# Two transformer blocks in one program: the ends of all four attention stages are rearranged

## The chip, the core and the metric

The kernel runs on one core of one Trainium2 chip. It is one straight program for five engines: TensorE (PE, matmuls; its weight loads are PEld), VectorE (DVE), ScalarE (ACT), GpSimd (POOL) and SyncE (SP, which issues the loads). The metric is device time in microseconds (us), the median of the runs; lower is better.

## The reference

256 tokens of width 1024, batch 1, float32 in and out, four layers in a row; every layer is x + mixer(norm(x)) and x + MLP(norm(x)):

```python
# layer "even": 8 heads of neighbourhood attention (64 wide, window and bias) and 8 heads
#   of latent attention (96 wide keys, 64 wide values); both concatenated, then @ ev_w_o
# layer "odd": dilated attention, 16 heads, 3 groups of keys each, merged in one softmax; @ od_w_o
# second block, layer 0: gated convolution (1024) and memory attention (4 heads of 128) over
#   256 memory tokens; concatenated (1536), @ a_w_out
# second block, layer 1: forgetting attention (8 causal heads of 128 with a bias) and memory
#   attention (4 heads); concatenated (1536), @ b_w_out
sc = einsum('bqhd,bkhd->bhqk', q, k) * scale     # each head
p = softmax(sc + bias)
o = einsum('bhqk,bkhd->bqhd', p, v)
x = x + concatenate(o over heads) @ w_o
x = x + square(relu(norm(x) @ w1)) @ w2          # first block
x = x + 0.5 * (silu(h @ w_gate) * (h @ w_up)) @ w_down   # second block, before and after each mixer
```

## The kernel before

**Weights.** All weights stream through the core once, in 299 chunks of 1 MB. A chunk is loaded into one of two slots of `W_raw`, and then split so that float32 products come out of faster matmuls: ACT rounds it to `W_hi` (`split_hi`, L1041), DVE subtracts to get `W_lo` (`split_lo`, L1308), each in two halves, and PE multiplies activations and weights as hi\*hi, hi\*lo, lo\*hi (`three`, L680 to L682). `ahead(g, slot)` splits chunk g+1 while chunk g is multiplied; `split_hi(g)` first waits until chunk g-2 has been multiplied (`chunk_done`). SP loads a chunk as soon as the raw slot has been split.

**Order.** A list of stages (`make_plan`) is walked by each engine's program in the same order; within a stage the order is the order of the code, and semaphores join the engines. Each engine executes its own queue strictly in order: a waiting instruction holds up all behind it.

**Down stages.** An output projection is a stage of kind "down": `ev_o` and `od_o` with 4 chunks, `a_out` and `b_out` with 6. Chunk j covers 256 of the rows of the weight. Its activations are staged in a slot of `SX` as hi (ACT, `stage_hi`, L1108) and lo (POOL, L1866). Its 24 matmuls accumulate in banks 4 to 7 of the accumulator memory PS: the first token half t = 0 in banks 4 and 5, the second half t = 1 in banks 6 and 7 (12 matmuls each, `down_chunk`).

**Attention stages.** There are four: "even" (16 heads in 8 pairs), "dilated" (16 heads in 8 pairs), "memory0" (4 heads), "fox" (12 heads, each a unit of its own). The steps of a unit, each named by its helper:

- `scores` (PE, L787 and L794): q times k into banks 4 to 7;
- `soft` (DVE, L1353, L1356 or L1371): row maxima, and the biased scores where there is a bias;
- `exps` (ACT, L1115): exponentials and their row sums;
- `normalise` (DVE, L1379 and L1382): reciprocals of the sums, and probabilities times them;
- `transposes` (PE, L811): probabilities through the identity matrix into the lower banks;
- `keep_pt` (ACT, L1125): the transposed probabilities copied out of PS;
- `values` (PE, L828 and L837): v times probabilities;
- `output` (DVE, L1394): the result copied to where the projection reads it.

The first units' scores and `soft` (`open_attention`) are issued inside the last chunk of the projection stage ahead, between its matmuls. The results of that last chunk are taken out of PS by DVE ("last eviction": L1593 in even, four L1639 in dilated, L1324 and L1333 in memory0 and fox). PE starts the attention stage proper with `pe.wait_ge(acc_read, u0)`, a wait for that eviction. In memory0 DVE's `open_attention` first waits for POOL's last gated product of the convolution (`conv_cu_done`), since a buffer is shared. The down stage starts after the last `values`; its second chunk is split then.

## Time and profile before

| | |
|---|---|
| median of 3 runs | 1855.12 us (1854.73 to 1856.68) |
| the profiled execution's own time | 1857.85 us |
| its span, first to last instruction | 1856.0 us |
| PE busy | 1811.1 us, 98% of the span |
| DVE busy | 1209.7 us, 65% |
| ACT busy | 929.9 us, 50% |
| POOL busy | 285.9 us, 15% |
| share of PE in the chain that ended last | 92% |
| mean granted clock of TensorE | 0.991 |

All durations of rows come from the profiled execution. A matmul's duration holds a pipelined tail, so the pace is read from the starts of rows, not from their durations. The granted clock is a share of 2.4 GHz; 0.50 is the lower level, 1.2 GHz.

### The profile page before, as it was taken

The page shows a single profiled execution, that of the slowest core. Times are in us where ns is not written, and L with a number is a line of the kernel's source. Part 1 is how long each engine was busy: PE and PEld are TensorE (multiplying, and loading weights), DVE is VectorE, ACT ScalarE, POOL GpSimd, SP SyncE. Part 2 cuts the span into 40 slices and gives each one's busy share as a digit, 9 for nine tenths or more (in the row PEclk, how much of TensorE's full clock was granted, in tenths as well). Part 3 has the DMA queues.
Part 4 walks back from the last instruction along what each step waited for, and adds up shares of the span by engine and source line. Part 5 has one row for each costly group of instructions (what it writes and reads, how often), then busy time and mean ns, then how long its engine had stood idle before and what let it go on. Part 6 is the DMA issues. An engine that isn't in the chain of part 4 may idle for free.

```text
span 1856.0 us, 27676 instructions
## 1 busy us (share of the span) xinstructions
PE 1811.1 (98%) x9835; PEld 1529.4 (82%) x9835; DVE 1209.7 (65%) x1536; ACT 929.9 (50%) x1396; POOL 285.9 (15%) x249
## 2 busy tenths in 40 slices
PE   9899999999989999999999989999999999899998
PEld 7678888888867888888888878888888888788886
DVE  6867745867876665566647756665667656656664
ACT  5465445434356444555545445454564445555543
POOL 1010021211201002110023920002000311020012
PEclk9899999999999999999999999999999999999999
DMA  6335555555523555555555535555556555245553
GB/s 222 109 131 182 182 198 171 174 181 183 180 92 103 182 182 202 189 174 189 194 187 178 189 129 181 181 189 196 182 174 209 184 186 187 81 148 184 193 188 136
DMA packets 215146, 320.19 MB, mean 173 GB/s; under 512 B 6040, under 2 KB 167072, under 8 KB 214944
## 3 DMA queue, kind: packets, MB, share of 16 engines
q1 hardware_dynamic: 214048, 315.80, 51.1%
q0 software_dynamic: 736, 3.15, 0.4%
q8 instruction: 48, 0.79, 0.2%
q10 hardware_dynamic: 288, 0.23, 0.0%
q14 instruction: 26, 0.21, 0.0%
HBM read 318.11 MB, written 1.06 MB: 172 GB/s over the span
## 4 chain that ended last, share of the span: by engine, by line
PE 92%; DVE 3%; ACT 2%; issue 1%; DMA 1%; POOL 0%; DVEq 0%; SPq 0%; POOLq 0%; ACTq 0%
PE PS L675 26%; PE PS L680 14%; PE PS L681 14%; PE PS L682 14%; PE PS L673 13%; PE PS L669 4%; PE PS L670 2%; PE PS L828 1%; PE PS L787 1%; DVE W_lo L1308 1%; PE PS L749 1%; PE PS L811 1%; DMA W_raw<-in_ev_w_in 1%; ACT U L1115 1%; ACT U L1125 1%
## 5 line engine op out<-in xcount | busy, mean ns | idle before, releaser
L1308 DVE TENSOR_TENSOR W_lo<-W_raw,W_hi 128x1024 fp32r<-128x1024 f32 x598 | 771.7, 1330 | 279.8 <-ACT W_hi L1041 258.1
L675 PE MATMUL PS<-XN,W_hi 128*128 128x512 f32 x2072 | 738.5, 396 | 0.0
L1041 ACT ACTIVATE W_hi<-W_raw 128x1024 fp32r<-128x1024 f32 x598 | 598.5, 1050 | 173.8 <-PE PS L682 116.8
L673 PE MATMUL PS<-XN,W_lo 128*128 128x256 f32 x2072 | 578.3, 279 | 0.0
L675 PEld LDWEIGHTS PS<-XN,W_hi 128*128 128x128 f32 x2072 | 388.8, 188 | 79.9
L673 PEld LDWEIGHTS PS<-XN,W_lo 128*128 128x128 f32 x2072 | 390.6, 189 | 13.5
L680 PE MATMUL PS<-W_hi,SX 128*128 128x512 f32 x780 | 305.1, 391 | 1.7 <-DVE W_lo L1308 1.7
L682 PE MATMUL PS<-W_hi,SX 128*128 128x512 f32 x780 | 303.8, 389 | 0.0
L681 PE MATMUL PS<-W_lo,SX 128*128 128x512 f32 x780 | 303.7, 389 | 0.0
L1866 POOL TENSOR_TENSOR SX<-U,SX 128x512 fp32r<-128x512 f32 (+1 forms) x98 | 128.6, 1316 | 1094.3 <-ACT SX L1108 1094.3
L1054 ACT ACTIVATE T<-PS 128x512 f32<-128x512 f32 x152 | 91.0, 599 | 405.2 <-PE PS L675 405.1
L1324 DVE TENSOR_TENSOR T<-PS,T 128x512 f32<-128x512 f32 x128 | 88.5, 691 | 213.6 <-ACT T L1054 213.6
L1108 ACT ACTIVATE SX<-U 128x512 fp32r (+2 forms) x98 | 60.5, 629 | 235.8 <-PE PS L682 232.3
L680 PEld LDWEIGHTS PS<-W_hi,SX 128*128 128x128 f32 x780 | 147.1, 189 | 32.7 <-issue 2.4
L681 PEld LDWEIGHTS PS<-W_lo,SX 128*128 128x128 f32 x780 | 147.1, 189 | 30.5
L682 PEld LDWEIGHTS PS<-W_hi,SX 128*128 128x128 f32 x780 | 146.8, 188 | 30.4
L680 PE MATMUL PS<-W_hi,XN 128*128 128x512 f32 (+1 forms) x352 | 138.5, 393 | 1.9 <-DVE W_lo L1308 1.2
L682 PE MATMUL PS<-W_hi,XN 128*128 128x512 f32 (+1 forms) x352 | 136.6, 388 | 0.0
L681 PE MATMUL PS<-W_lo,XN 128*128 128x512 f32 (+1 forms) x352 | 136.6, 388 | 0.0
L669 PE MATMUL PS<-XN,W_hi 128*128 128x512 f32 x296 | 118.6, 401 | 1.2 <-DVE XN L1338 1.2
L670 PE MATMUL PS<-XN,W_lo 128*128 128x256 f32 x296 | 82.2, 278 | 0.0
L680 PEld LDWEIGHTS PS<-W_hi,XN 128*128 128x128 f32 x352 | 66.1, 188 | 17.3 <-DVE W_lo L1308 3.3
(169 smaller groups left out, 1499.7 us busy)
## 6 DMA issues: line engine op xcount, KB each, us to landing
W_raw<-in_ffn_w_gate_up SPq DMA_DIRECT2D x88, 1024.0 KB, 5.1
W_raw<-in_mlp_w SPq DMA_DIRECT2D x64, 1024.0 KB, 5.2
W_raw<-in_ffn_w_down SPq DMA_DIRECT2D x44, 1024.0 KB, 4.9
W_raw<-in_od_w_in SPq DMA_DIRECT2D x36, 1024.0 KB, 5.1
W_raw<-in_a_w_in SPq DMA_DIRECT2D x14, 1024.0 KB, 5.0
W_raw<-in_mem_w_kv SPq DMA_DIRECT2D x8, 1024.0 KB, 5.1
W_raw<-in_w_kvf SPq DMA_DIRECT2D x8, 1024.0 KB, 5.4
W_raw<-in_ev_w_in SPq DMA_DIRECT2D x6, 1024.0 KB, 5.3
```

What stands on the lines that cost most here:

```text
L669: mm(bank, wT(W_hi, slot, k, fb), both, start=True, stop=False)
L670: mm(bank[:, S:], wT(W_lo, slot, k, fb), xn[:, k, 0, :], start=False, stop=False)
L673: mm(bank[:, S:], wT(W_lo, slot, k, fb), xn[:, k, 0, :], start=False, stop=False)
L675: last = mm(bank, wT(W_hi, slot, k, fb), both, start=False, stop=k == KD - 1)
L680: mm(bank, xh, wh, start=start, stop=False)
L681: mm(bank, xh, wl, start=False, stop=False)
L682: return mm(bank, xl, wh, start=False, stop=stop)
L1041: A(W_hi[:, slot, halves(h)], W_raw[:, slot, halves(h)], ACT.Copy).then_inc(w_hi, 1)
L1054: A(T0[:, pair, :].rearrange("p (f t) -> p f t", f=2), PS[:, 2 * pair:2 * pair + 2, S:2 * S], ACT.Copy, scale=times).then_inc(cross_out, 1)
L1308: V.tensor_tensor(W_lo[:, slot, halves(h)], W_raw[:, slot, halves(h)], W_hi[:, slot, halves(h)], ALU.subtract).then_inc(w_lo, 1)
L1324: return V.tensor_tensor(dst.rearrange("p (f t) -> p f t", f=2), PS[:, 2 * pair:2 * pair + 2, 0:S], T0[:, pair, :].rearrange("p (f t) -> p ...
L1866: nc.gpsimd.tensor_tensor(SX[:, slot, 1, 0:st["ks"] * S], down_src(st, j), SX[:, slot, 0, 0:st["ks"] * S], ALU.subtract).then_inc(st_lo, 1)
```

## The change

1. **Opening.** DVE normalises the first two heads before it does the last eviction. ACT computes their exponentials before its own part: in even and dilated ACT now evicts the second half of the last result (`v_kept`), DVE the first. PE's wait for the eviction moves from the front of the stage to just ahead of the first `values`; to allow it, transposes use the banks that the last projection does not occupy (`free`), `values` the others (`taken`).
2. **Interleaving.** The first chunk of the output projection is multiplied inside the attention stage, in two halves of 12 matmuls (`down_half`): in even and dilated both halves between the last units' steps, in memory0 and fox three halves (chunk 0 twice, chunk 1 once; the fourth follows the stage). So `stage_early` stands further ahead on ACT, and chunk 1 is split within the stage.
3. **Around it.** In memory0 the first two chunks of `a_out` are staged in the stage ahead (ACT), and POOL makes their lo part before the last quarter of the convolution. `soft` of heads 2 and 3 waits for the convolution's product there, no longer heads 0 and 1. The order of ACT and DVE within even changes: ACT does the exponentials of units 1 and 2 after unit 0 is kept and before unit 1 is kept. The loops of the four down stages are written out.

```diff
+                late = (st["u"] - 1) % 2
+                st["free"], st["taken"] = 2 - 2 * late, 2 * late
...
-            def down_chunk(st, g, staged, slot, first, final):
+            def down_chunk(st, g, staged, slot, first, final, tiles=range(TT), last_half=True):
...
+            def down_half(st, j, t, last_half):
+                down_chunk(st, st["g"] + j, st["staged0"] + j + 1, (st["g"] + j) % 2, j == 0,
+                           j == st["n"] - 1, (t,), last_half)
...
                 elif kind == "attend":
-                    pe.wait_ge(acc_read, u0)
...
+                    def accumulators_read():
+                        pe.wait_ge(acc_read, u0)
+                        if st["paired"]:
+                            pe.wait_ge(v_kept, st["v_kept"])
+                    if st["name"] == "even":
+                        for u in us:
+                            for n_ in units[u]:
+                                transposes(n_)
+                            if u + 2 in us:
+                                scores(u + 2)
+                            if u == us[0]:
+                                accumulators_read()
+                            if u >= us[-2]:
+                                down_half(then, 0, u % 2, u == us[-1])
+                            values(u)
+                    elif st["name"] == "dilated":
+                        for u in us:
+                            if u + 1 in us:
+                                scores(u + 1)
+                            else:
+                                pe.wait_ge(s_soft, a0 + m)
+                                down_half(then, 0, 0, False)
+                            transposes(units[u][0])
+                            if u == us[0]:
+                                accumulators_read()
+                            transposes(units[u][1])
+                            if u == us[-1]:
+                                down_half(then, 0, 1, True)
+                            values(u)
...
@@ ACT, even
+                        exps_unit(us[0])
+                        act.wait_ge(chunk_done, g0)
+                        A(region(R["na_v"] + 512, 512), PS[:, st["taken"] + 1, :], ACT.Copy,
+                          scale=rstd_of(1)).then_inc(v_kept, 1)
+                        keep_unit(us[0])
+                        exps_unit(us[1])
+                        exps_unit(us[2])
+                        for u in us[1:]:
+                            keep_unit(u)
+                            exps_unit(u + 2)
+                            if u == us[-4]:
+                                stage_early(then)
+                            if u == us[-2]:
+                                ahead(then["g"], then["g"] % 2)
...
@@ DVE, open_attention
-                if st["name"] == "memory0":
-                    dve.wait_ge(conv_cu_done, 4)
                 soft(st["a0"])
                 soft(st["a0"] + 1)
+                normalise(st["a0"])
+                normalise(st["a0"] + 1)
...
@@ DVE, memory0
+                        second_chunk()
+                        dve.wait_ge(conv_cu_done, 4)
+                        soft_unit(us[2])
+                        soft_unit(us[3])
+                        output(us[0])
+                        output(us[1])
+                        normalise_unit(us[2])
+                        normalise_unit(us[3])
...
@@ POOL, convolution
+                        if c == 3:
+                            for j in range(2):
+                                slot = (then["g"] + j) % 2
+                                pool.wait_ge(st_hi, then["staged0"] + j + 1)
+                                Pg.tensor_tensor(SX[:, slot, 1, :], down_src(then, j), SX[:, slot, 0, :],
+                                                 ALU.subtract).then_inc(st_lo, 1)
```

What this makes of the queues is shown at three places. First DVE at the start of the even stage, before (ISA rows are `soft`, L1593 is the last eviction, L1379 and L1382 are `normalise`):

```order
L1371 ISA U,ST<-PS,U 128x256
L1371 ISA ST 128x1
L1593 TENSOR_SCALAR U<-PS,ST 128x512 x2
L1371 ISA U,ST<-PS,U 128x256
L1371 ISA ST 128x1
...
L1379 RECIPROCAL ST<-ST 128x2
L1382 TENSOR_SCALAR U<-U,ST 128x256 x2
```

and after (L1490 is `soft`, L1498 and L1501 `normalise`, L1712 the eviction):

```order
L1490 ISA U,ST<-PS,U 128x256
L1490 ISA ST 128x1
L1498 RECIPROCAL ST<-ST 128x2
L1501 TENSOR_SCALAR U<-U,ST 128x256 x2
L1498 RECIPROCAL ST<-ST 128x2
L1501 TENSOR_SCALAR U<-U,ST 128x256 x2
L1712 TENSOR_SCALAR U<-PS,ST 128x512
L1490 ISA U,ST<-PS,U 128x256
```

The two normalisations moved ahead of the eviction and of the second unit's `soft`, and the eviction is one instruction, not two.

Second, PE in memory0 from the end of the last projection to the first matmul of `a_out`, before (L787 scores, L811 transposes, L828 values):

```order
L787 MATMUL PS<-U 128x256 x2
L811 MATMUL PS<-K,T 128x128 x4
L787 MATMUL PS<-U 128x256 x2
L828 MATMUL PS<-U 128x256 x2
L811 MATMUL PS<-K,U 128x128 x4
L828 MATMUL PS<-U 128x256 x2
L811 MATMUL PS<-K,U 128x128 x4
L828 MATMUL PS<-U 128x256 x2
L811 MATMUL PS<-K,T 128x128 x4
L828 MATMUL PS<-U 128x256 x2
L680 MATMUL PS<-W_hi,SX 128x512
```

and after (L824 transposes, L800 scores, L841 values, L691 to L693 the halves of chunks 0 and 1, 12 matmuls each):

```order
L824 MATMUL PS<-K,U 128x128 x8
L691 MATMUL PS<-W_hi,SX 128x512
...
L800 MATMUL PS<-U 128x256 x4
L841 MATMUL PS<-U 128x256 x4
L691 MATMUL PS<-W_hi,SX 128x512
...
L824 MATMUL PS<-K,T 128x128 x4
L824 MATMUL PS<-K,U 128x128 x4
L691 MATMUL PS<-W_hi,SX 128x512
...
L841 MATMUL PS<-U 128x256 x4
```

Between any two groups of attention work that depend on each other through ACT or DVE there now stand 12 matmuls of the projection.

Third, POOL at the last quarter of the convolution, before (L1907 the gated product, L1914 and L1918 the taps, L1919 the result):

```order
L1919 TENSOR_TENSOR U<-U 128x512
L1907 TENSOR_TENSOR U<-T 128x2x256
L1914 TENSOR_SCALAR U<-U,G 128x256 x4
L1918 TENSOR_TENSOR U<-U 128x512
L1914 TENSOR_SCALAR U<-U,G 128x256 x2
```

and after (L2061 the lo parts of the first two chunks of `a_out`):

```order
L2076 TENSOR_TENSOR U<-U 128x512
L2061 TENSOR_TENSOR SX<-U,SX 128x512 x2
L2064 TENSOR_TENSOR U<-T 128x2x256
L2071 TENSOR_SCALAR U<-U,G 128x256 x4
L2075 TENSOR_TENSOR U<-U 128x512
```

The two subtractions, and with them a wait for ACT's staging, stand ahead of the last product and all of its taps.

## Rows read from the trace of the kernel before

**Rows 1.** Timeline, even, PE: start, duration, engine, line, operation, count, idle before

```profile
73.64 0.39 PE L682 MATMUL PS<-W_hi,XN 128*128 128x512 f32 x1
77.80 1.94 PE L811 MATMUL PS<-K,U 128*128 128x128 f32 x8 [3.76 <-DVE U L1382]
...
83.53 1.09 PE L811 MATMUL PS<-K,U 128*128 128x128 f32 x8
...
85.70 1.08 PE L828 MATMUL PS<-U 128*64 128x256 f32 x8
...
105.58 1.08 PE L828 MATMUL PS<-U 128*64 128x256 f32 x8 [1.84 <-ACT U L1125]
...
108.52 1.08 PE L828 MATMUL PS<-U 128*64 128x256 f32 x8 [0.83 <-ACT U L1125]
109.54 0.50 PE L680 MATMUL PS<-W_hi,SX 128*128 128x512 f32 x1
```

**Rows 2.** Windows: length, busy of PE, PEld, DVE, ACT, POOL, clock, DMA

```profile
74.03:109.54 35.51, 28.49 (x178) 19.76 (x177) 26.34 (x97) 24.66 (x78) 2.50 (x2) 0.90 0.06 25
528.11:576.14 48.03, 40.28 (x569) 31.08 (x568) 34.34 (x115) 32.13 (x92) 2.63 (x2) 0.93 0.02 8
1068.15:1081.23 13.08, 7.93 (x41) 5.99 (x41) 7.83 (x21) 7.55 (x21) 5.68 (x5) 1.00 0.06 23
1596.10:1629.71 33.61, 27.32 (x128) 21.63 (x129) 21.44 (x79) 20.31 (x61) 2.49 (x2) 0.85 0.00 1
...
1599.00:1602.36 3.36, 3.35 (x12) 2.95 (x13) 2.25 (x11) 1.51 (x5) 0.00 (x0) 0.50 0.00 0
1622.84:1629.30 6.46, 5.58 (x15) 4.44 (x16) 1.45 (x3) 2.49 (x3) 1.64 (x2) 0.50 0.01 3
```

**Rows 3.** Timeline, even, ACT: exponentials and copies of transposed probabilities

```profile
74.23 0.18 ACT L1115 ACTIVATION_READ_ACCUMULATOR U<-U,ST 128x1 f32 x1
...
82.60 0.51 ACT L1115 ACTIVATE U<-U,ST 128x256 f32<-128x256 f32 x1 [2.23 <-DVE ST L1371]
...
84.59 1.06 ACT L1125 ACTIVATE U<-PS 128x512 f32<-128x512 f32 x2
```

**Rows 4.** Timeline, even, DVE: the first head's normalisation

```profile
77.04 0.61 DVE L1382 TENSOR_SCALAR U<-U,ST 128x256 f32<-128x256 f32 x2
```

**Rows 5.** Timeline, dilated, PE

```profile
527.72 0.39 PE L682 MATMUL PS<-W_hi,XN 128*128 128x512 f32 x1
...
537.49 1.08 PE L828 MATMUL PS<-U 128*64 128x256 f32 x8 [0.35 <-ACT U L1125]
...
538.97 1.13 PE L787 MATMUL PS<-U 64*128 64x256 f32 x8
...
542.86 1.08 PE L828 MATMUL PS<-U 128*64 128x256 f32 x8 [0.41 <-ACT U L1125]
...
572.04 0.87 PE L811 MATMUL PS<-K,T 128*128 128x128 f32 x6 [0.81 <-DVE T L1382]
...
574.67 1.08 PE L828 MATMUL PS<-U 128*64 128x256 f32 x8 [0.46 <-ACT U L1125]
...
576.14 0.50 PE L680 MATMUL PS<-W_hi,SX 128*128 128x512 f32 x1
```

**Rows 6.** Timeline, a_out, ACT: staging released by the ends of two chunks

```profile
1087.26 0.63 ACT L1108 ACTIVATE SX<-U 128x512 fp32r x1 [5.03 <-PE PS L682]
...
1092.70 0.63 ACT L1108 ACTIVATE SX<-U 128x512 fp32r x1 [2.91 <-PE PS L682]
```

**Rows 7.** Timeline, memory0, DVE normalising a head

```profile
1070.49 1.43 DVE L1382 TENSOR_SCALAR T<-T,ST 128x256 f32<-128x256 f32 x2
```

**Rows 8.** Timeline, memory0, POOL's last step of the convolution

```profile
1069.91 1.59 POOL L1919 TENSOR_TENSOR U<-U 128x512 f32<-128x512 f32 x1
```

**Rows 9.** Waits of PE, fox: total us, times, longest

```profile
PE PS L811 <- DVE U L1333: 2.9, 1, 2.9
PE PS L828 <- ACT U L1125: 2.8, 3, 1.2
```

More of the change, by code:

```diff
@@ L348, in build_program @@
         bias_ready = sem("bias_ready")
+        v_kept = sem("v_kept")
         dve_chain, pool_chain = sem("dve_chain"), sem("pool_chain")
@@ L723, in down_chunk @@
                 chunk_ready(g, 0 if by_half else 1)
-                for t in range(TT):
-                    if first and t == 1 and st["src"] == "h" and not st["each"]:
-                        pe.wait_ge(h_done, st["h0"])
+                for t in tiles:
                     steps = [(ks, b) for ks in range(ks_n) for b in range(2)]
@@ L730, in down_chunk @@
                     for at, (ks, b) in enumerate(order):
-                        if by_half and t == 0 and ks and not any(k for k, _ in order[:at]):
+                        if by_half and t == tiles[0] and ks and not any(k for k, _ in order[:at]):
                             chunk_ready(g, 1)
@@ L1012, in _ @@
                     a0, m = st["a0"], len(st["what"])
[L1014 to L1029 removed]
+                    us, then = st["units"], st["next_down"]
@@ L1275, in _ @@
                     a0, m = st["a0"], len(st["what"])
-                    if stages[stages.index(st) - 1]["kind"] != "up":
-                        exps(a0)
-                    exps(a0 + 1)
-                    if st["name"] == "even":
-                        exps(a0 + 2)
-                        exps(a0 + 3)
-                    lead = 2 if st["name"] in ("memory0", "fox", "even") else 1
-                    for u in st["units"]:
+                    us, then = st["units"], st["next_down"]
```

218 lines of the change are left out of this document (157 added, 61 removed).

## The prediction

> **What bounds the kernel now.** I read the shares of busy time first: PE is busy for 98% of the span and makes up 92% of the chain that ended last. So only PE's own idle time, and time in which its clock is low, can be won. Next came the granted clock by stretches, then PE's waits and its timeline in the four attention stages. These stages take 35.5, 48.0, 13.1 and 33.6 us with PE busy for 28.5, 40.3, 7.9 and 27.3 us [rows 2]: 26.2 us idle in 130. Their mean clock is 0.90, 0.93, 1.00 and 0.85. Even, dilated and fox each open with a long wait, followed by work at 0.50: even waits 3.76 us for the first normalisation, which stands behind the eviction on DVE [rows 1]; fox waits 2.9 us and then works at 0.50 for 3.4 us [rows 2, 9]. The ends look alike: the last units have no further scores to cover ACT's copy, so PE waits 1.84 and 0.83 us in even [rows 1], 0.81 and 0.46 us in dilated [rows 5], and in fox the clock falls again for 6.5 us, into the first down chunk [rows 2].
>
> The work of PE is the same after the change: the half chunks only stand elsewhere. The sum is therefore what goes of waits and low clock, less new waits. A chunk takes 5.44 us (the ends of two chunks, 1087.26 and 1092.70 [rows 6]), a half 2.7 us.
>
> **Even.** The last projection matmul ends at 74.03 (73.64 and its 0.39 [rows 1]). ACT's exponentials of the first two heads end at 74.4 already [rows 3]. Normalising a head is a reciprocal and two multiplies, 0.8 us by my estimate with the 0.61 of the two multiplies in it [rows 4]; the second head is ready at 75.2 and, with the 0.15 us from there to PE (77.04 plus 0.61 to 77.80 [rows 1, 4]), its transposes go at 75.4. Transposes and scores take 2.17 us in all (83.53 to 85.70 [rows 1]), of which about 0.5 are the second head's transposes; so the first values start near 76.9. The eviction, one half on each engine, is over by then.
>
> Then the order on ACT costs something. ACT keeps unit 0 until 76.9 (1.06 [rows 3]), computes unit 1 until 78.9 (four exponentials are 1.99, 82.60 to 84.59 [rows 3]), DVE normalises until 79.7 and only then does unit 2's `soft`, whose first head is ready some 0.7 us later; ACT computes unit 2 from 80.4 to 82.4, and only then keeps unit 1, until 83.5. PE, queued behind, waits at the transposes (about 1.4 us) and at the values of unit 1 (2.3 us), which start at 83.5 instead of 85.70 [rows 1]. So of 3.76 us of wait and the low clock 2.2 us are left as gain. At the end 1.84 and 0.83 go, covered by a half chunk each, and moving the staging ahead of a keep that PE is waiting for costs its 1.06 us (two copies at 0.53; the 0.63 of rows 6 has a tail). Sum: 2.2 + 2.67 - 1.06 = **3.8 us**. Bounds: 2.1 if the low clock returns in these waits (below), 8.9 if none of the new waits came.
>
> **Dilated.** The last matmul ends at 528.11 and the first values start at 537.49 [rows 5]. Afterwards scores, transposes and values follow at once, with both heads normalised and the eviction shared between DVE and ACT (about 1.5 us each, four half-height instructions divided by two). In the next unit the way from scores to values is 3.89 us (538.97 to 542.86, its wait of 0.41 included [rows 5]), so the values start near 532.1: 5.4 us won. The repeated part stays as it is. At the end 0.81 and 0.46 go behind two half chunks: 1.3 us. Sum **6.7 us**; bounds 5.5 (one more 1.2 us wait for the second head) and 7.5.
>
> **Memory0.** 13.08 us with 7.93 busy [rows 2]: 5.15 us of waits, and a half chunk now stands between every pair of steps that wait for each other. The wait for chunk 1's split is covered: ACT starts it near 70, DVE ends near 73.5, PE comes to it near 76. What may stay is the DVE's pace. POOL's last product and taps now start after staging and two subtractions, some 9 us later, and run beside DVE's normalisations. The row that shows such a meeting: two multiplies take 1.43 us beside POOL's 1.59 us instruction [rows 7, 8], where they take 0.61 alone [rows 4]. For the two heads that PE waits for at the front that is up to 1.6 us, of which I take 0.35, since the product is nearly over. Sum **4.8 us**; bounds 1.9 (each of the four normalisations slowed by 0.8) and 5.2.
>
> The Trainium skill ("SBUF — State Buffer", section "Who interferes with whom") says that VectorE in its two-port modes and GpSimd take one pair of ports as a lock, and that the one that comes second is blocked until the first ends. The trace agrees for the one meeting above: the multiplies end 0.4 us after POOL's instruction. By the rule every normalisation in memory0 could be held by one instruction of POOL, which would take the sum to the lower bound just named; by the row alone it stays near 4.8.
>
> **Fox.** Waits of 2.9 and 2.8 us [rows 9]; at 0.50 the work in the two low stretches, 3.35 and 5.58 us busy [rows 2], takes twice as long, so half of 8.93, 4.5 us, is lost there. Together 10.2 us. New: unit 2 has neither its maxima nor its probabilities ahead, since they stand behind the eviction, `soft` of units 2 and 3 and one set of exponentials on ACT: about 1.2 us of wait, and 0.3 us at the first head. At the end three half chunks, 8.2 us, cover the copies and the split of chunk 1. Sum **8.7 us**; bounds 5.9 (the second fall of the clock stays) and 9.9.
>
> **Edits at nothing.** The written-out loops add no work. POOL's later convolution ends near 82; its result is wanted by the staging of chunk 3, near 87. Chunk 2 of each projection is split when chunk 0 is done, up to one half chunk and one values step before PE needs it; in memory0 its first half is ready about 1 us early. If that cover were gone it would cost 1 us a stage. Chunk 3 is loaded earlier than before, into a DMA queue that is idle in these stages (0.00 to 0.06 busy [rows 2]).
>
> **Sum.** 3.8 + 6.7 + 4.8 + 8.7 = 24.0 us. Against the profiled execution: span 1856.0 to 1832.0, and with the 1.85 us around it (1857.85 less 1856.0) 1833.85. That execution was 2.73 us above the median; from the median 1855.12 the same gain gives **1831.1 us**.
>
> **The rivals.**
> - *The clock falls in even all the same.* For it: in fox it fell at 1622.84 after waits of no more than 1.2 us each [rows 2, 9], and even now has waits of 0.9, 0.5 and 2.3 us close together. Against: memory0, idle for 5.15 of 13.08 us, stayed at 1.00 [rows 2]. Price: 3.4 us at 0.50 lose 1.7, 6.5 us lose 2.8 (half the busy time of the two stretches [rows 2]). Time 1832.8 to 1833.9. The Trainium skill ("TensorE: Matmul & The Clock Gate", section "A second HAM failure mode: psum-queue depth-cycling") tells of a kernel whose frequent short idles between groups of matmuls made the clock go down and up; the row of fox agrees, that of memory0 does not.
> - *POOL slows memory0* to its lower bound: 2.9 us less, 1834.0. With the one above 1836 to 1837.
> - *Only the ends are won.* Were the first values no earlier in any stage (another wait, the eviction say, in place of the normalisation), what remains is 2.7 - 1.1 in even, 1.3 in dilated, half of the 5.15 in memory0, and 2.8 of waits plus 2.8 of clock in fox: 11 us, 1844. Against it: the eviction ends ahead of the first values in each walk above.
> - *Slower: the half chunks run at the low clock.* If the changed rhythm keeps the clock at 0.50 where they stand, each of the ten halves costs 2.7 us more, 27 us, against 24 won: 1858. It decides from the point at which nine of ten halves are hit. Against it: a half chunk is solid work, and the clock came back to 1.00 after 3.4 and 6.5 us each time [rows 2].
>
> **Chances.** Forecast 0.57; clock in even 0.17; POOL 0.12, either alone or with the clock; only the ends 0.06; slower 0.02; the rest, 0.06, for more won than worked out (fewer new waits in even and fox, up to 4 us). About 0.2% (3.7 us) is what a measurement of this kernel can tell from no change. Faster by more 0.95, within 0.03, slower 0.02. The range takes in both clock and POOL at its upper end, 1837.5, and the rest at its lower end, 1827.0.
>
> **What the profile after would show.** Right: the four stages, from the last projection matmul to the first matmul of the remaining down stage, less the half chunks, at about 31.7, 41.3, 8.3 and 24.9 us (rows 2 less the sums); no wait above 0.6 us before the first values; a granted clock of 1.00 in dilated and fox; in even two waits near 80 and 82, of some 1.4 and 2.3 us, the second for ACT's copy. Wrong: a wait of PE for POOL's or ACT's staging ahead of a half chunk; chunk 2 late behind DVE's last output; a clock of 0.50 beside half chunks; first values where they were.

## The result, and the profile after

The changed kernel takes **1833.3 us** (median of 4 runs, 1832.19 to 1833.82), the kernel before on the same chip 1855.9 us (4 runs, 1854.73 to 1859.20). The ratio is 0.9875, 95% interval 0.986 to 0.989: 1.25% faster, inside the range given, 2.2 us above the forecast of 1831.1.

The profiled execution took 1833.31 us, with a span of 1831.5 us: 24.5 less than before. PE is busy for 1800.1 us of it, where it was busy for 1811.1. The matmuls are the same 9835, so most of these 11.0 us are matmuls that no longer run at half clock; the other 13.5 are idle time of PE. Of the 11.0, 1.4 lie between 50 and 60 us, where even starts no earlier for it (73.91 against 74.03). In the four attention stages the gain is 9.9 us of half clock and 14.4 of idle time.

The four attention stages as in [rows 2], from the end of the last projection matmul to the first matmul of the down stage that is left (columns as there):

```profile
73.91:112.24 38.33, 33.26 (x200) 23.67 (x200) 28.03 (x96) 26.86 (x81) 2.52 (x3) 0.96 0.07 25
525.32:571.59 46.27, 43.08 (x592) 33.25 (x592) 34.07 (x112) 35.46 (x96) 3.11 (x3) 1.00 0.08 26
1058.15:1075.52 17.37, 15.67 (x77) 12.81 (x77) 11.74 (x22) 8.59 (x21) 11.73 (x10) 1.00 0.26 99
1582.24:1612.34 30.10, 28.21 (x161) 24.37 (x159) 21.11 (x73) 20.30 (x59) 2.83 (x3) 1.00 0.10 36
```

The stages are longer by the half chunks that now stand in them (2.72 us each: two in even and dilated, three in memory0 and fox). PE's idle time in them is 5.07, 3.19, 1.70 and 1.89 us; it was 7.02, 7.75, 5.15 and 6.29. The clock of the first is 0.96, of the others 1.00. Less the half chunks:

| stage | before | forecast | after | won, forecast | won, measured |
|---|---|---|---|---|---|
| even | 35.51 | 31.7 | 32.89 | 3.8 | 2.6 |
| dilated | 48.03 | 41.3 | 40.83 | 6.7 | 7.2 |
| memory0 | 13.08 | 8.3 | 9.21 | 4.8 | 3.9 |
| fox | 33.61 | 24.9 | 23.05 | 8.7 | 10.6 |

In fox [rows 2] reach four matmuls into the first down chunk, some of them at half clock; the table goes to the same matmul after, at 1613.45. The stages sum to 24.3 of the 24.5 us: nothing of weight happened outside them.

Even after, PE; the rows answer to [rows 1]:

```profile
73.52 0.39 PE L693 MATMUL PS<-W_hi,XN 128*128 128x512 f32 x1
74.20 0.66 PE L824 MATMUL PS<-K,U 128*128 128x128 f32 x4 [0.29 <-DVE U L1501]
...
76.83 1.08 PE L841 MATMUL PS<-U 128*64 128x256 f32 x8
78.51 0.66 PE L824 MATMUL PS<-K,U 128*128 128x128 f32 x4 [0.59 <-DVE U L1501]
...
83.24 1.11 PE L841 MATMUL PS<-U 128*64 128x256 f32 x8 [2.03 <-ACT U L1198]
...
112.24 0.51 PE L691 MATMUL PS<-W_hi,SX 128*128 128x512 f32 x1
```

The first values of the kernel before, to compare with the row at 76.83:

```profile
81.67 1.93 PE L828 MATMUL PS<-U 128*64 128x256 f32 x8
```

The wait of 3.76 us is gone; the first values start 2.92 us after the projection's end (7.64 before). But those of unit 1 wait 2.03 us for ACT's copy, L1198. And fox, where [rows 9] had 2.9 us in front and 2.8 at the end:

```profile
1584.44 0.92 PE L841 MATMUL PS<-U 128*128 128x256 f32 x4 [0.24 <-DVE U L1452]
1586.95 0.66 PE L824 MATMUL PS<-K,T 128*128 128x128 f32 x4 [1.59 <-DVE T L1501]
```

These two are all the waits of the stage that are long enough to be listed; the end has none. In dilated the first values start 3.85 us after the projection's end at 525.32:

```profile
529.17 1.08 PE L841 MATMUL PS<-U 128*64 128x256 f32 x8 [0.45 <-ACT U L1198]
```

Memory0 keeps three waits, all for DVE's normalisation (L1501):

```profile
1058.89 0.66 PE L824 MATMUL PS<-K,U 128*128 128x128 f32 x4 [0.74 <-DVE U L1501]
1059.82 0.66 PE L824 MATMUL PS<-K,U 128*128 128x128 f32 x4 [0.27 <-DVE U L1501]
...
1070.01 0.66 PE L824 MATMUL PS<-K,T 128*128 128x128 f32 x4 [0.61 <-DVE T L1501]
```

### The profile page after: what moved, and what is told of

The parts are those of the page before. It is cut to its first block, busy times and chain, and to the rows that moved or that the text cites. A ratio compares the mean times of both kernels' runs of the same rounds, so it can differ in the third digit from the quotient of the medians.

```text
span 1831.5 us, 27590 instructions
## 1 busy us (share of the span) xinstructions
PE 1800.1 (98%) x9835; PEld 1523.3 (83%) x9835; DVE 1209.1 (66%) x1533; ACT 932.5 (51%) x1399; POOL 285.5 (16%) x249
## 3 DMA queue, kind: packets, MB, share of 16 engines
HBM read 318.11 MB, written 1.06 MB: 174 GB/s over the span
## 4 chain that ended last, share of the span: by engine, by line
PE 92%; DVE 4%; ACT 2%; issue 1%; DMA 1%; POOL 0%; DVEq 0%; ACTq 0%; POOLq 0%
PE PS L686 26%; PE PS L691 14%; PE PS L693 14%; PE PS L692 14%; PE PS L684 13%; PE PS L680 4%; PE PS L681 2%; DVE W_lo L1427 2%; PE PS L841 1%; PE PS L800 1%; PE PS L762 1%; PE PS L824 1%; ACT U L1188 1%; PE PS L961 1%; ACT U L1198 0%
## 5 line engine op out<-in xcount | busy, mean ns | idle before, releaser
L1427 DVE TENSOR_TENSOR W_lo<-W_raw,W_hi 128x1024 fp32r<-128x1024 f32 x598 | 771.3, 1329 | 264.6 <-ACT W_hi L1111 242.5
L684 PEld LDWEIGHTS PS<-XN,W_lo 128*128 128x128 f32 x2072 | 391.0, 189 | 13.5
L691 PE MATMUL PS<-W_hi,SX 128*128 128x512 f32 x780 | 305.1, 391 | 1.8 <-DVE W_lo L1427 1.7
L693 PE MATMUL PS<-W_hi,SX 128*128 128x512 f32 x780 | 303.3, 389 | 0.0
L691 PEld LDWEIGHTS PS<-W_hi,SX 128*128 128x128 f32 x780 | 146.5, 188 | 32.5 <-issue 2.4
L693 PEld LDWEIGHTS PS<-W_hi,SX 128*128 128x128 f32 x780 | 146.5, 188 | 30.3
L691 PE MATMUL PS<-W_hi,XN 128*128 128x512 f32 (+1 forms) x352 | 138.6, 394 | 3.4 <-issue 1.5
L693 PE MATMUL PS<-W_hi,XN 128*128 128x512 f32 (+1 forms) x352 | 136.7, 388 | 0.0
L691 PEld LDWEIGHTS PS<-W_hi,XN 128*128 128x128 f32 x352 | 66.1, 188 | 18.7 <-DVE W_lo L1427 3.3
```

The lines of the kernel that those rows point to most:

```text
L684: mm(bank[:, S:], wT(W_lo, slot, k, fb), xn[:, k, 0, :], start=False, stop=False)
L691: mm(bank, xh, wh, start=start, stop=False)
L693: return mm(bank, xl, wh, start=False, stop=stop)
L1427: V.tensor_tensor(W_lo[:, slot, halves(h)], W_raw[:, slot, halves(h)], W_hi[:, slot, halves(h)], ALU.subtract).then_inc(w_lo, 1)
```

## The experiments

All are edits of the changed kernel; u is a unit, us the units of a stage. Since one edit moves the time by less than the runs scatter, I read each first from the length of its stages. Stage lengths less the half chunks in them, to the first matmul of the down stage in fox too (31.57 before):

| kernel | even | dilated | memory0 | fox | median us |
|---|---|---|---|---|---|
| changed | 32.89 | 40.83 | 9.21 | 21.94 | 1833.3 |
| changed, again | 31.45 | 40.87 | 9.22 | 21.92 | 1833.51 |
| opening only | 36.18 | 42.51 | 14.51 | 22.73 | 1842.35 |
| ends only | 33.84 | 45.23 | 13.92 | 24.46 | 1845.73 |
| even, both edits | 29.31 | 40.86 | 9.19 | 23.59 | 1831.38 |
| fox without lead | 31.48 | 40.83 | 9.23 | 24.99 | 1835.7 |
| without taps | 31.47 | 40.86 | 8.47 | 21.94 | 1831.43 |
| fox, three heads | 31.48 | 40.86 | 9.23 | 20.12 | 1831.1 |
| memory0 staged earlier | 32.89 | 40.85 | 7.93 | 21.93 | 1832.86 |
| filler matmuls | 31.47 | 40.85 | 9.22 | 23.64 | 1832.91 |
| even and fox | 29.27 | 40.87 | 9.23 | 20.11 | 1828.40 |
| all three edits | 29.29 | 40.85 | 7.93 | 20.16 | 1827.49 |

Where an edit does not touch a stage, the length repeats to 0.05 us, except for two jumps: even 31.5 or 32.9, and fox 21.9 or 23.6. Both are the clock: it is 0.96 in the even of 32.9 us and 1.00 in that of 31.5, 0.95 in the fox of 23.6 us and 1.00 in that of 21.9.

### The changed kernel again

No edit.

> The changed kernel itself once more. What is open is whether the half clock of 3.4 us in even (1.7 us lost, from 84.2 us on) belongs to the kernel or to the single execution: the same instructions of that stage in the run without the lead in fox showed the same waits and full clock. If it belongs to the waits (2.03 us at 83), it falls again at the same place; if it is of the execution, it may fall there or not, with even at 31.5 or 32.9 us, and the time stays within 1832 to 1834.5.

The times were 1832.23 to 1833.92. The window 80 to 90 us, first in the trace of the changed kernel, then in this one (columns as above):

```profile
80.00:90.00 10.00, 7.97 (x45) 5.69 (x44) 7.20 (x31) 6.40 (x21) 0.00 (x0) 0.83 0.00 0
```

```profile
80.00:90.00 10.00, 7.74 (x55) 5.54 (x54) 8.20 (x36) 7.56 (x27) 0.00 (x0) 1.00 0.00 0
```

With the same instructions and the same wait (2.04 us at 83) the clock was 0.83 once and 1.00 once: so the fall belongs to the execution and not to the kernel alone. 0.83 over ten microseconds are 3.4 us at half speed, and the stage pays 1.44 us for them. Of the seven traces that left this place unedited, it fell there in three (changed, opening only, memory0 staged earlier).

### Opening only

```diff
-                            if u >= us[-2]:
-                                down_half(then, 0, u % 2, u == us[-1])
...
-                            if u == us[-4]:
-                                stage_early(then)
                             if u == us[-2]:
-                                ahead(then["g"], then["g"] % 2)
+                                stage_early(then)
+                        ahead(then["g"], then["g"] % 2)
```

and so in all four stages.

> The changed kernel with the half chunks undone: the first down chunk or chunks of each following stage, ACT's split and staging and DVE's second chunk go back behind the last heads; the heads normalised ahead of the last eviction, ACT's eviction of the second half and the transposes of fox one unit ahead stay. Theory (the two parts save apart, at the two ends of each stage, and add): the end waits of before come back, about 2.5 us in even, 1.5 in dilated, 2.5 in memory0 and 3.5 in fox, 10 in all, so about 1843 us, with the first values of every stage where the changed kernel has them (3.3 us after the stage's start in even, 3.9 in dilated). Rival (the half chunks are worth nothing of their own, the opening does it all): stages within 0.5 us of the changed kernel's, about 1834. Second rival (the parts need each other, since a gap at either end drops the clock): over 14 us slower, about 1848.

1842.35 us (1840.13 to 1844.21; ratio to before 0.9909, 0.9891 to 0.9928), 9 us above the changed kernel, near the 10 of the first theory. The parts are distributed otherwise. Memory0, first wait and last values:

```profile
1072.84 0.66 PE L824 MATMUL PS<-K,T 128*128 128x128 f32 x4 [3.18 <-DVE T L1478]
...
1074.27 3.57 PE L841 MATMUL PS<-U 128*128 128x256 f32 x8
```

DVE's normalisation of head 2 is waited for with 3.18 us (0.61 with a half chunk in front of it), and the eight values behind it take 3.57 where they take 1.89 at full clock: 5.3 us in that stage, twice what I expected. In even the wait of 1.84 us at the end is back, and behind it another 3.4 us at half clock. Fox loses only 0.8, against 3.5 expected. Its end has one wait, though no half chunk covers it now:

```profile
1612.91 0.66 PE L824 MATMUL PS<-K,T 128*128 128x128 f32 x4 [0.40 <-DVE T L1478]
```

So something other than the half chunks removes most of the 2.8 us of end waits of fox.

### Ends only

```diff
-                normalise(st["a0"])
-                normalise(st["a0"] + 1)
...
-                        for t in range(1 if st.get("next_attend") else TT):
+                        for t in range(TT):
...
-                        act.wait_ge(chunk_done, g0)
-                        A(region(R["na_v"] + 512, 512), PS[:, st["taken"] + 1, :], ACT.Copy,
-                          scale=rstd_of(1)).then_inc(v_kept, 1)
```

> The changed kernel with the opening undone: the first heads are normalised behind the last eviction, DVE evicts both halves, PE waits for both before its first attention work; the half chunks between the last heads' steps and the transposes of fox one unit ahead stay. Theory: the start waits of before come back, in dilated the 5.4 us that its stage saved at the front, in even 1 to 3.5 (the front wait comes back, but the clock that fell there in the changed kernel may stay up), in memory0 about 2.3, in fox 2.9 and up to 1.7 of half clock behind it: 12 to 14 us, so 1845 to 1847 us. Rival (the end waits carry the gain): under 5 us slower, 1838. In fox the steady period of three units stays 5.44 us, since the transposes one unit ahead are still there; if it goes back to 6.31, what shortened it was the opening.

1845.73 us (1845.36 to 1847.15; ratio 0.9933, 0.9915 to 0.9951), 12.4 above the changed kernel. The front waits are back, in memory0 with 3.65 us:

```profile
1067.15 1.09 PE L824 MATMUL PS<-K,U 128*128 128x128 f32 x4 [3.65 <-issue]
1068.73 1.11 PE L824 MATMUL PS<-K,U 128*128 128x128 f32 x4 [0.49 <-DVE U L1491]
```

The groups of four transposes take 1.1 us instead of 0.66: half clock behind the wait. Nine of the twelve matmuls of the half chunk behind them are slow too (0.43 us from start to start instead of 0.23): a half chunk does not bring the clock back at once. The total is as expected, but memory0 loses 4.7 us, twice the 2.3 expected, and dilated 4.4 for 5.4. Three units of fox take 5.44 us here too, so the opening is not what shortened them.

The two parts alone win 13.6 and 10.2 us from the 1855.9 of the first comparison, 23.8 together, where the whole wins 22.6. Against the kernel before as it ran beside them (1858.1) they win 15.7 and 12.3, 28.0 together. The transposes of fox one unit ahead are in both and count twice (2 to 3 us, next experiment), which leaves 21 to 26. So each part wins by itself, but whether they add up exactly these times do not decide, and no run separates the pieces of the opening (normalising first, the shared eviction, the later wait of PE).

### Fox without the lead

In the changed kernel PE issues the transposes of unit u + 1 and the scores of unit u + 4 ahead of the values of unit u. The loop of before did not:

```diff
-                        transposes(a0)
-                        scores(us[3])
...
-                            if u + 1 in us:
-                                transposes(units[u + 1][0])
-                            if u + 4 in us:
-                                scores(u + 4)
+                            transposes(units[u][0])
+                            if u + 3 in us:
+                                scores(u + 3)
```

> The changed kernel with the transposes of fox in their own unit again (one wait for the exps is added ahead of one half chunk), everything else kept. Theory (in the kernel before each unit of fox waited some 0.29 us for ACT's keep inside the step from transposes to values, too short for the list of waits, and the transposes one unit ahead hide it): the steady period of three units goes from 5.44 back to about 6.3 us, +2.6 us over nine units, about 1836. Rival (the period was shortened by the clock or by waits at the front that the opening took away): the period stays at 5.44 and the time within 0.5 us of 1833.

1835.7 us (1834.57 to 1836.52), 2.2 to 2.4 above; fox is 3.05 us longer. Two values steps in a row in the steady part, PE; first the changed kernel, then this one:

```profile
1591.14 0.82 PE L800 MATMUL PS<-U 128*128 128x128 f32 x4
1591.79 0.82 PE L841 MATMUL PS<-U 128*128 128x256 f32 x4
1592.45 0.60 PE L824 MATMUL PS<-K,T 128*128 128x128 f32 x4
1592.88 1.03 PE L800 MATMUL PS<-U 128*128 128x256 f32 x4
1593.75 0.82 PE L841 MATMUL PS<-U 128*128 128x256 f32 x4
```

```profile
1590.27 0.82 PE L800 MATMUL PS<-U 128*128 128x128 f32 x4
1591.21 0.89 PE L841 MATMUL PS<-U 128*128 128x256 f32 x4
1591.94 0.60 PE L824 MATMUL PS<-K,T 128*128 128x128 f32 x4
1592.38 1.03 PE L800 MATMUL PS<-U 128*128 128x256 f32 x4
1593.32 1.10 PE L841 MATMUL PS<-U 128*128 128x256 f32 x4
```

From scores to values 0.94 us pass without the lead, 0.65 with it, and no row shows an idle time (between the end of the scores and the values 0.12 us are left). ACT's row in that step, from the same trace:

```profile
1590.47 0.60 ACT L1196 ACTIVATE U<-PS 128x512 f32<-128x512 f32 x1 [0.49 <-PE PS L824]
```

ACT's copy ends at 1591.07 and the values that read it start at 1591.21, while the scores before them are over. With the lead the copy has been made a unit earlier. The period of three units is 6.31 us (1587.01 to 1593.32), against 5.44 in the changed kernel, and as in the kernel before (1605.67 to 1611.98):

```profile
1605.67 1.10 PE L828 MATMUL PS<-U 128*128 128x256 f32 x4
...
1611.98 1.10 PE L828 MATMUL PS<-U 128*128 128x256 f32 x4
```

The theory stands. Of the 3.05 us, 1.12 are listed waits (1.22, 0.33, 0.62 and 0.78 here against 0.24 and 1.59); the other 1.9 are 0.29 us a unit over some seven units. At the end of the stage two of the waits come back, 0.62 us ahead of a half chunk and this one:

```profile
1612.87 1.10 PE L841 MATMUL PS<-U 128*128 128x256 f32 x4 [0.78 <-ACT U L1196]
```

So of the 2.8 us at the end of fox the half chunks without the lead leave 1.40, and the lead without the half chunks left 0.40.

### Even, both edits

```diff
+                        exps_unit(us[1])
                         act.wait_ge(chunk_done, g0)
...
-                        exps_unit(us[1])
...
-                            exps_unit(u + 2)
-                            if u == us[-4]:
+                            if u == us[-3]:
                                 stage_early(then)
+                            exps_unit(u + 2)
...
+                if st["name"] == "even":
+                    soft(st["a0"] + 2)
+                    soft(st["a0"] + 3)
```

> The changed kernel with two edits in the stage even alone: the softmax and the exps of unit 1 are done ahead of the last eviction, and ACT's early staging stands one exps earlier, between keep(5) and exps(7). Theory: the second values waited 2.03 us for ACT's keep of unit 1 behind exps of unit 1, and 1.3 of it go; the wait of 1.15 at the early staging goes to 0 to 0.2; and if the clock does not fall at 84 us, 1.7 more: even shorter by 2.3 to 4.0 us (from 32.9 less its half chunks), 1829.5 to 1831. Rival (ACT's chain in front is only moved ahead of the eviction, which then comes later): the first values come 0.7 later and the sum is -1.0. Second rival for the clock: the gap of 2 us is not what lowers it, and the half clock shows in even also where the wait is gone.

Even is 29.31 us, 3.6 shorter than in the first trace and 2.15 shorter than at full clock. PE:

```profile
75.04 1.38 PE L824 MATMUL PS<-K,U 128*128 128x128 f32 x8 [1.11 <-DVE U L1501]
...
77.96 1.08 PE L841 MATMUL PS<-U 128*64 128x256 f32 x8 [0.47 <-ACT U L1198]
...
81.63 1.08 PE L841 MATMUL PS<-U 128*64 128x256 f32 x8 [0.50 <-ACT U L1198]
...
102.86 1.08 PE L841 MATMUL PS<-U 128*64 128x256 f32 x8 [0.39 <-ACT U L1198]
```

The 2.03 us became 0.50, at the price of first values 1.1 us later (4.02 us after the start; the rival's part, with 0.7 expected), and the 1.15 us at the early staging became 0.39. But the time fell only to 1831.38 (1829.50 to 1831.60), and the trace shows why: in this execution the clock was low in fox, which took 23.59 instead of 21.94 (without the three half chunks that stand in the length below):

```profile
1578.67:1610.42 31.75, 29.86 (x160) 25.65 (x159) 21.15 (x73) 20.32 (x59) 2.83 (x3) 0.95 0.11 34
```

### Fox with three heads ahead

```diff
+                                if st["next_attend"]["name"] == "fox":
+                                    exps(st["next_attend"]["a0"] + 2)
...
+                if st["name"] == "fox":
+                    soft(st["a0"] + 2)
...
+                if st["name"] == "fox":
+                    normalise(st["a0"] + 2)
```

> The changed kernel with one edit in fox alone: head 2 as well gets its softmax, exps and normalisation ahead of the last eviction (three heads instead of two). Theory (the 1.59 us in front of the transposes of head 2 wait for DVE's normalisation, which stands behind the eviction and its split only by its place in the queue): the wait goes, or 0.3 of it is left, fox less its half chunks goes from 21.9 to 20.4 us, about 1831.8. Rival (DVE is late in front anyway, so head 2's work delays the eviction and head 0): the same 1.5 us show up as a wait in front of the first values and fox stays at 21.9.

1831.1 us (1830.22 to 1831.76). The window of fox, to be read against the fourth row above:

```profile
1581.21:1609.49 28.28, 27.97 (x160) 24.32 (x159) 19.79 (x69) 19.40 (x55) 2.83 (x3) 1.00 0.11 38
```

0.31 us idle of 28.28: the wait of 1.59 is gone and nothing took its place. The theory stands to 0.3 us (20.12 for 20.4).

### Memory0 without the last taps, and with earlier staging

```diff
-                        for tap in (2, 1, 0):
+                        for tap in (2, 1, 0) if c < 3 else ():
```

> The changed kernel without the taps of POOL's convolution in its last quarter (six multiply-adds of the last quarter are left out, so its sum is not formed); everything else kept. Theory (POOL's multiply-adds slow DVE's rows beside them): DVE's split L1427 at 1062 takes 2.35 instead of 3.38 us, the normalisation that PE waits for last comes earlier and the wait of 0.61 goes: memory0 0.6 shorter, about 1832.7; the waits of 0.74 and 0.27 in front stay, since the subtractions of L2061 run there. Rival (DVE is slowed by PE's and ACT's accesses, or by its own operands' layout): the row stays at 3.4 us and memory0 at 9.2. Second rival (a POOL row of one kind slows DVE and of the other not): the rows beside L2061 stay slow and those beside L2071 are as slow as alone already.

DVE's second split in memory0 (L1427) and the normalisation that PE waits for last, with POOL's taps beside the split; the changed kernel:

```profile
1063.35 3.73 POOL L2071 TENSOR_SCALAR U<-U,G 128x256 f32<-128x256 f32 x2
...
1062.09 3.38 DVE L1427 TENSOR_TENSOR W_lo<-W_raw,W_hi 128x1024 fp32r<-128x1024 f32 x2 [1.01 <-ACT W_hi L1111]
...
1067.84 2.12 DVE L1501 TENSOR_SCALAR T<-T,ST 128x256 f32<-128x256 f32 x2
```

and without the taps:

```profile
1060.99 2.36 DVE L1427 TENSOR_TENSOR W_lo<-W_raw,W_hi 128x1024 fp32r<-128x1024 f32 x2 [1.00 <-ACT W_hi L1111]
...
1066.16 0.62 DVE L1501 TENSOR_SCALAR T<-T,ST 128x256 f32<-128x256 f32 x2
```

The split loses 1.02 us and the normalisation 1.50 to POOL. The last wait of PE goes, memory0 is 0.74 shorter (0.6 expected), and the front waits 1.30 where it waited 0.74 and 0.27: POOL's subtractions and product are still there. The theory stands. The second experiment moves them:

```diff
+                            if kind == "up" and s == 0 and st.get("next_attend", {}).get("name") == "memory0":
+                                stage_early(st["next_attend"]["next_down"])
...
-                                if st["next_attend"]["name"] == "memory0":
-                                    stage_early(st["next_attend"]["next_down"])
```

> The changed kernel with one edit ahead of memory0: ACT's early staging (the subtraction operands that POOL waits for) stands one chunk of the up projection earlier. Theory (what slows DVE in memory0, 3.4 us for a row that takes 2.35 alone, and the waits of 0.74, 0.27 and 0.61 of PE, are POOL's rows beside it, and POOL began when ACT's staging came, its wait of 6.85 us): POOL is done some 5 us earlier, the last wait of 0.61 goes and the front loses half: memory0 less its half chunks from 9.2 to 8.2 us or a bit over, about 1832.3. Rival (POOL's rows only move and meet other DVE rows of the up projection, whose splits feed PE): memory0 shortens, but the same time is lost ahead of it, and the total does not move. Second rival (ACT's staging delays ACT's own work there): a wait of PE of up to 2.7 us appears ahead of memory0, 1835.

```profile
1053.09 1.99 PE L800 MATMUL PS<-U 128*128 128x256 f32 x8 [1.69 <-DVE U L1452]
...
1060.06 0.66 PE L824 MATMUL PS<-K,U 128*128 128x128 f32 x4 [0.35 <-DVE U L1501]
...
1069.85 0.66 PE L824 MATMUL PS<-K,T 128*128 128x128 f32 x4 [0.20 <-DVE T L1501]
```

Memory0's waits fall from 1.62 to 0.55 us and the stage by 1.28, but the wait for the first scores, ahead of it, grows from 0.89 to 1.69. The distance from the end of dilated to the start of memory0 is 487.35 us here and 486.55 in the repetition. Net 0.5: the theory holds for the stage, the first rival for the account. The median moved by 0.4 to 0.7, which these runs alone would not show. POOL's two last taps L2071 take 2.46 us here, beside two short rows of DVE (0.69 us each), and 3.73 beside the split: both engines are slowed where they meet, not the later one alone. The split itself is not faster here but slower, beside POOL's last two rows of 1.29 and 2.13 us:

```profile
1062.33 4.48 DVE L1427 TENSOR_TENSOR W_lo<-W_raw,W_hi 128x1024 fp32r<-128x1024 f32 x2 [0.90 <-ACT W_hi L1111]
```

What shortens the last wait to 0.20 us is the normalisation behind it, which is back at 0.62 us.

The Trainium skill ("SBUF — State Buffer", section "Who interferes with whom") says that a VectorE instruction with two operands in SBUF, such as this split, contends with a GpSimd instruction that reads SBUF. The runs agree: 3.38 us with the taps, 2.36 without.

### Filler matmuls in the gap

```diff
+                        def filler(n):
+                            for _ in range(n):
+                                mm(PS[:, st["taken"] + 1, :], XN[:, 0, 0, 0:P], both_halves(XN, 0),
+                                   start=True, stop=True)
...
+                            if u == us[1]:
+                                filler(7)
```

> The changed kernel with seven extra matmuls whose result is not used, on PE, in the wait of 2.03 us ahead of the values of unit 1 in even; seven of these take 1.6 us at 0.23 us each. In the traces of that stage so far, with the same wait of 2.03 to 2.04 us, the clock fell behind it in three of seven and stayed at full in four. Theory (the idle gap is what lets the clock fall): with the gap filled it does not fall in even, the values start where they did, 9.3 us after the stage's start, and even is 36.9 us long; the times are 1832.2 to 1832.6 more often than 1833.3 to 1833.9. Rival (the gap has nothing to do with it): the half clock shows at 84 us in this trace too, or the times keep their mean of 1833.2. Second rival (the extra matmuls cost by themselves, since they end after the keep is ready): the values start up to 0.4 later.

```profile
81.27 1.91 PE L1045 MATMUL PS<-XN 128*128 128x512 f32 x7
83.38 1.08 PE L841 MATMUL PS<-U 128*64 128x256 f32 x8 [0.20 <-ACT U L1204]
```

The gap is filled and the values are not late. The clock stayed at 1.00 in even, as the theory wants, but so it did in four of seven traces with the gap. The times (1831.96, 1832.07, 1833.75, 1833.96) fall in the same two groups as without filler, since the clock fell in fox instead in the profiled execution. By itself it did not settle the cause. In even the clock was low behind the gap of 2.0 us in 3 of 7 traces, and in none of the 4 without that gap (both edits, even and fox, all three, filler); in fox it was low in 2 of 7 with the wait of 1.59 us, and in none of 3 without it. Such splits are weak: falls spread over the traces at random would give the first one time in five, the second one time in two.

The thirteen traces hold more, if every wait of PE above 1 us from 45 us on is set beside the clock. All low stretches, but for the one at the very end of the program, begin in such a wait or within 1.4 us behind it:

| wait of PE, us | waits | clock fell behind |
|---|---|---|
| 1.11 to 1.15 | 11 | 0 |
| 1.22 to 1.30 | 3 | 1 |
| 1.52 to 1.84 | 19 | 3 |
| 2.03 to 2.29 | 21 | 8 |
| 2.91 to 3.77 | 8 | 8 |

So the clock falls behind waits, the more often the longer they are, and behind each of the longest, which in the kernel before stood at the front of even, dilated and fox (3.76, 3.14 and 2.91 us). These are counts of thirteen executions and no rule.

### The edits together

> The same without the edit of memory0: even and fox alone. Theory: even 34.75, fox 28.3, memory0 as in the changed kernel at 17.4: 1829.4, 0.4 to 0.5 above the three together. Rival (the earlier staging of memory0 is worth its whole 1.3 us, and the 0.8 lost ahead of it in the single run was a half clock): 1830.3, 1.3 above. The clock: where the wait of 2.0 us at 83 us is gone, it does not fall in even in this trace either.

> The changed kernel with the three edits together: both softmaxes of units 0 and 1 and their exps ahead of the eviction in even and its staging one exps earlier, three heads ahead in fox, and the early staging of memory0 one chunk earlier. Theory (they act in different stages and add, at full clock): even 36.9 to 34.75, fox 30.1 to 28.3, memory0 17.4 to 16.1 less 0.8 lost ahead of it: 4.4 us below the 1833.4 of the changed kernel, 1829.0. Rival (the clock takes back part of it: each trace so far lost 0, 1.7 or 3.4 us in one or two stretches, and a stage saved may start one elsewhere): 1830.5 to 1831.5.

Even and fox: 1828.40 us (1827.59 to 1828.96; ratio to before 0.9843, 0.9829 to 0.9856). All three: **1827.49 us** (1827.41 to 1827.93; 0.984, 0.9826 to 0.9853), 5.8 below the changed kernel, the best version run. The windows of all three, in the stages' order:

```profile
73.85:108.58 34.73, 31.62 (x201) 22.57 (x201) 28.06 (x92) 26.52 (x81) 2.55 (x3) 1.00 0.08 27
521.70:567.99 46.29, 43.10 (x592) 33.22 (x592) 34.02 (x112) 35.46 (x96) 3.13 (x3) 1.00 0.08 26
1055.33:1071.42 16.09, 15.49 (x76) 12.57 (x75) 10.58 (x19) 7.99 (x17) 6.69 (x6) 1.00 0.24 84
1578.16:1606.48 28.32, 28.01 (x160) 24.33 (x159) 19.79 (x69) 19.40 (x55) 2.83 (x3) 1.00 0.11 38
```

They add: 4.4 us were expected, and from the 1832.2 us that the changed kernel takes where its clock stays up, 4.5 us (2.2 in even, 1.8 in fox, 1.3 less 0.8 in memory0) lead to 1827.7. The clock is 1.00 in all four stages. The expected 0.4 between the two kernels was 0.9, but their intervals overlap, so the times do not say which theory holds for the edit of memory0. The two traces do: memory0 is 1.30 us shorter with it, and the stretch ahead is 487.33 us with it and 486.53 without, both at a clock that fell nowhere in it. So the 0.8 lost ahead is no half clock, the rival fails, and 0.5 of the 0.9 between the medians is the edit's. What is left idle in these four stages is 3.1, 3.2, 0.6 and 0.3 us, 7.2 in all, against 26.2 before the change.

## Why the prediction was right, and where it was off

- **The mechanism was right**: PE bounds, its work is constant, both ends of each stage give. The two parts alone win 13.6 (opening) and 10.2 us (ends) from 1855.9, and 15.7 and 12.3 from the kernel before beside them.
- **The sum was right in part by luck.** Against the 24.0 us of the forecast the stages won 24.3, but they differ by -1.2, +0.5, -0.9 and +1.9, which cancel. Without the gain in fox that nobody forecast, the sum would have been 22.4.
- **Even, 3.8 forecast, 2.6 measured.** The walk through ACT's queue held: first values forecast at 76.9, measured 76.83; values of unit 1 forecast 83.5, measured 83.24, behind 2.03 us of wait (2.3 forecast); early staging 1.06 forecast, 1.15 measured. The transposes of unit 1 waited 0.59 and 0.33 instead of 1.4. What is missing is the clock, 1.4 us: the first rival happened in this execution, at a price just under its 1.7. At full clock, in the repetition, the stage won 4.1.
- **Dilated, 6.7 and 7.2.** First values forecast 4.0 us after the start, measured 3.85 (529.17 less 525.32). At the end I had counted 0.81 and 0.46 of [rows 5]; a third wait between them, 0.32 us at 573.23 in the kernel before, went as well.
- **Memory0, 4.8 and 3.9.** The term that was mis-sized is POOL beside DVE: I took 0.35 us of waits as left and 1.62 are (0.74, 0.27, 0.61). I had priced a meeting at 0.8 us and charged it to the two heads at the front alone; the split lost 1.02 us and the third normalisation 1.50, which the experiment without taps shows. The POOL rival came true by 0.9 of its 2.9 us. The stage is short of the forecast by less than the 1.27 us of added waits, since PE's work without the half chunks takes 7.51 us in it and not 7.93; why stays open.
- **Fox, 8.7 and 10.6.** The new waits are 1.83 (0.24 and 1.59), as forecast within 0.3 (1.5). The step that failed is "the repeated part stays as it is", written for dilated and used here without being said: the change reorders fox's loop (which its description in three points does not name), and the lead wins some 2 us by hiding ACT's copy. I read the loop's waits from the list of waits, where this one has no row, and did not compare the order of the steps with their distances in time. At the end, too, the lead does more than the three half chunks to which I gave the 2.8 us: each alone would leave 0.40 and 1.40 of it.
- **Edits at nothing** held: no wait of PE for a split stands in the four stages, and no half chunk of the changed kernel ran at low clock.
- **The signs.** "No wait above 0.6 us before the first values" failed in memory0 (0.74). The two waits of unit 1 in even came at 78.5 and 83.2 us; the first was 0.92 us in two pieces, not 1.4.
- **The rivals.** The ends alone, with fox's reordered loop, win 10.2 to 12.3 us, about the 11 that I had for "only the ends". The clock in even is real, but a matter of the single execution, in 3 of 7, not of the kernel. The rival on the slower side, half chunks at half clock, did not show in the changed kernel; with the ends alone nine matmuls of one half chunk were slow.
- **The last step, from the profile to the median, cost the 2.2 us.** Against the profiled execution I forecast 1833.85 and it was 1833.31. Then I took the same 24.0 us off a median 2.73 us lower. But 10 of the 24.5 us are half clock that was in the profiled execution, and a faster execution of before has less of it to give: of its 26 later runs the nine fastest (1854.6 to 1856.8) have a mean granted clock of 0.994 or 0.995, all others 0.990 to 0.992. Later medians of the kernel before are 1855.9, 1858.1, 1856.2, 1858.1 and 1858.2, its runs 1854.6 to 1860.9; the eight of the changed kernel lie within 1.8 us. The change removes a scatter as much as a wait.

The Trainium skill ("TensorE: Matmul & The Clock Gate", section "A second HAM failure mode: psum-queue depth-cycling") tells of clock changes from frequent short idles between groups of matmuls. In this case each fall lies behind a wait of 1.2 to 3.8 us, in places with shorter ones close ahead of it (0.59 and 0.33 before the 2.03 in even, 0.78 before the 1.22 in fox in the kernel before). Where waits above 1.2 us are gone, none came, but the same waits of 2.0 us left the clock up in four of seven traces, so the runs agree in part and do not decide how far the rule carries.

## What to carry to other kernels

Walk each stage's queues by durations; it gave the first values and those of unit 1 in even to 0.3 us. Do it for the loop's steady part too, wherever the order in it changes, and compare the distance between dependent steps with the work that stands between them: a loss of 0.29 us in each of a dozen units had no row here. When part of the gain is low clock, take it from several executions of before, not from one profile and another execution's median.

## What the runs showed of the hardware

- The same instructions with the same waits ran at full clock in one execution and had 3.4 us at half clock in another (1.44 us on a stage of 36.9, 1.65 to 1.7 in fox); the two groups of times, 1.35 and 1.84 us apart in the mean, fit it. A low stretch between 50 and 60 us, in five of the thirteen traces, did not show in the time: even starts at 73.85 to 74.13 with one and at 73.56 to 74.38 without.
- Behind all eight waits of PE of 2.91 to 3.77 us the granted clock fell, behind 8 of 21 of 2.03 to 2.29 us, and behind none of 11 of 1.11 to 1.15 us.
- DVE's subtraction of two tiles of 128 x 1024 took 2.36 us alone, 3.38 beside POOL's multiply-adds and 4.48 beside two of its `TENSOR_TENSOR` rows of 128 x 512; a pair of the multiply-adds took 3.73 beside it and 2.46 beside shorter rows.
- ACT's copy, ready just behind the end of the matmuls ahead, cost PE 0.29 us a step in fox; it shows only in the distance of the starts (0.94 against 0.65 us).
